# Two stacked models on one core: gates and branches of the first model computed by token, their bias rows loaded by DMA, the mix turned by feature

## The reference

```
proj = rms_norm(h) @ w_in[l]            # ..., gate_pre: 3 x 1024 columns
y_a = dsa_attention(...); y_b = short_conv_mixer(...); y_c = rwkv7_time_mix(...)
up    = einsum('bsgc,gcd->bsgd', stack([y_a, y_b, y_c]), w_branch[l])   # 512 -> 1024, three times
gates = sigmoid(gate_pre + b_gate[l])                                    # three gates of 1024
mixed = sum(gates * up, over the three branches)
h = h + mixed @ w_out[l]
h = h + conv_glu_ffn(rms_norm(h), ...)
```

## Time and profile before

| | |
|---|---|
| median of three runs | 1637.47 us |
| the profiled execution | 1637.91 us, span 1636.0 us |
| TensorE busy | 1620.9 us, 99% |
| VectorE busy | 1233.5 us, 75% |
| ScalarE busy | 966.8 us, 59% |
| POOL busy | 384.9 us, 24% |
| chain that ended last | TensorE 77%, VectorE 16%, ScalarE 4% |
| slabs | 143 of the first model, 104 of the second, median 4.9 us to landing |

### The profile page before, as it was taken

The page is one execution under the profiler, slowest core; times in us unless marked ns, Lnnn a source line. Parts: engine busy times, 40 slices in busy tenths (PEclk is TensorE's granted clock), DMA queues, the critical chain, the costliest instruction groups (busy, mean ns, idle before and its releaser), DMA issues.

```text
span 1636.0 us, 27673 instructions
## 1 busy us (share of the span) xinstructions
PE 1620.9 (99%) x11270; PEld 1409.2 (86%) x11270; DVE 1233.5 (75%) x1663; ACT 966.8 (59%) x1525; POOL 384.9 (24%) x291
## 2 busy tenths in 40 slices
PE   9999999999999999999999999999999999999998
PEld 7989999988888989999988888778788888787786
DVE  7987447699988975547799887779866668788664
ACT  7684525556567575345655574565684555656753
POOL 0663400000001945100000006508200056083000
PEclk9999999999999999999999999999999999999999
DMA  7443633455545424525465555434445555345352
GB/s 279 170 155 110 194 105 134 176 184 193 191 173 203 159 104 157 166 90 185 147 230 183 203 172 196 172 129 158 160 146 181 185 199 176 130 154 175 134 180 77
DMA packets 49182, 270.63 MB, mean 165 GB/s; under 512 B 13664, under 2 KB 14688, under 8 KB 17312
## 3 DMA queue, kind: packets, MB, share of 16 engines
q1 hardware_dynamic: 38736, 265.71, 46.5%
q10 hardware_dynamic: 9712, 2.62, 0.7%
q0 software_dynamic: 608, 0.53, 0.2%
HBM read 267.01 MB, written 1.84 MB: 164 GB/s over the span
## 4 chain that ended last, share of the span: by engine, by line
PE 77%; DVE 16%; ACT 4%; issue 2%; DMA 1%; SPq 0%; DVEq 0%; ACTq 0%
PE bank L1812 11%; PE bank L1813 11%; PE bank L1817 11%; PE bank L1704 7%; DVE w_low L1076 6%; PE bank L2866 6%; PE bank L1749 5%; PE bank L1750 5%; PE bank L1754 5%; PE bank L1709 3%; PE bank L2871 3%; PE bank L2904 2%; ACT w_high L621 1%; ACT arena L722 1%; DVE arena L1275 1%
## 5 line engine op out<-in xcount | busy, mean ns | idle before, releaser
L1076 DVE TENSOR_TENSOR w_low<-slab,w_high 128x2048 fp32r<-128x2048 f32 (+1 forms) x249 | 595.8, 2401 | 170.2 <-ACT w_high L621 163.1
L621 ACT ACTIVATE w_high<-slab 128x2048 fp32r<-128x2048 f32 (+1 forms) x249 | 470.6, 1896 | 106.5 <-PE bank L1817 88.6
L1812 PE MATMUL bank<-w_high,act 128*128 128x512 f32 x864 | 343.7, 398 | 1.4 <-DVE act L1239 0.7
L1813 PE MATMUL bank<-w_high,act 128*128 128x512 f32 x864 | 337.1, 390 | 0.0
L1749 PE MATMUL bank<-act,w_high 128*128 128x256 f32 x1024 | 258.7, 290 | 0.0
L1750 PE MATMUL bank<-act,w_high 128*128 128x256 f32 x1024 | 251.8, 283 | 0.0
L1817 PE MATMUL bank<-w_low,act 128*128 128x512 f32 x864 | 240.9, 389 | 0.0
L2416 POOL TENSOR_TENSOR arena<-arena 128x512 f32<-128x512 f32 x32 | 60.6, 1894 | 626.3 <-DVE arena L2685 626.3
L1749 PEld LDWEIGHTS bank<-act,w_high 128*128 128x128 f32 x1024 | 195.8, 191 | 8.3 <-issue 5.6
L1750 PEld LDWEIGHTS bank<-act,w_high 128*128 128x128 f32 x1024 | 196.2, 192 | 0.5 <-issue 0.5
L1812 PEld LDWEIGHTS bank<-w_high,act 128*128 128x128 f32 x864 | 162.4, 188 | 39.7 <-issue 7.4
(11 more groups left out here) (271 smaller groups left out, 2336.9 us busy)
## 6 DMA issues: line engine op xcount, KB each, us to landing
slab<-stream_a SPq DMA_DIRECT2D x143, 1024.0 KB, 4.9
slab<-stream_b SPq DMA_DIRECT2D x104, 1024.0 KB, 4.9
arena<-x_t SPq DMA_DIRECT2D x4, 256.0 KB, 6.6
slab<-stream_a ACTq DMA_DIRECT2D x2, 512.0 KB, 6.1
residual<-x_tok SPq DMA_DIRECT2D x1, 1024.0 KB, 11.5
lora_weights<-lora SPq DMA_DIRECT2D x2, 512.0 KB, 7.9
lora_weights<-final_rows SPq DMA_DIRECT2D x2, 512.0 KB, 5.9
d_inverse<-arena ACTq DMA_DIRECT2D x2, 256.0 KB, 2.2
```

The costliest lines, as they stand in the source:

```text
L621: line.did(eng.activation(core.wh[u % PARTS][:, 0:SLAB_WIDTH[u]], core.slab[u % SLABS][:, 0:SLAB_WIDTH[u]], ACT.Copy), core.sem("slab_high"))
L1076: line.did(line.eng.tensor_tensor(core.wl[u % PARTS][:, 0:SLAB_WIDTH[u]], core.slab[u % SLABS][:, 0:SLAB_WIDTH[u]], core.wh[u % PARTS][:, ...
L1812: eng.matmul(out, core.xh[:, at, columns_], wh[:, k, :], start=first and k == 0, stop=False, skip_group_check=True)
L1813: eng.matmul(out, core.xl[:, at, columns_], wh[:, k, :], start=False, stop=False, skip_group_check=True)
```

## The change

- Gate and branch slabs hold a block of 512 features by rows (`rows_by_block`) and are multiplied by token (`tokens_half`, as `out_half` does). Two gate slabs, half of the depth each, make a pair (six pairs per layer, `GATE_BLOCKS`) with two banks; a branch slab has its whole depth of 512 and two banks.
- By token the bias is a row. Six times per layer SyncE loads the pair's row, repeated over the partitions (256 KB), into the first half of `lora_weights`, behind the slab that comes five after the pair's first (`gate_rows_to`), once the last pair's banks are emptied.
- VectorE adds bank and row into the arena (`bias`), 128 x 512 twice per pair. For five of the six pairs this is the second slab's unit step, and its slab is now in `late`: the addition stands in front of the round and split two on. The first pair's is put behind mask 3.
- ScalarE's sigmoid is a step of its own (`gate`), arena to arena, 128 x 512 twice per pair.
- VectorE's products and sums of the branches keep their number and size.
- The mix is by token and is turned: TensorE turns 4 groups of 4 tiles (`mix`), two groups amid br2's second slab and two amid out's first; ScalarE and VectorE write high and low from the banks. `by_depth` is left to the FFN.

```
+BIASED = [(kind, 2 * half + 1) for kind, half in GATE_BLOCKS[1:]]
+
+
 def plan(units):
 
...
-        fills = 2 - 2 * i if kind in ("q", "w") else 2 if kind.startswith("br") else 0 if kind in ("down", "out") else 1
-        parts = 1 if kind == "up" else 1 + i if kind in ("q", "w") else 1 + i % 2 if kind == "out" else 4 if (kind, i) == ("down", FT // 2 - 1) else max(fills, 1)
-        reader = "act" if kind in ("q", "w", "rz", "ga", "gb", "gc") else "dve"
+        fills = 2 - 2 * (i % 2) if kind in ("q", "w") + GATES else 2 if kind.startswith("br") else 0 if kind in ("down", "out") else 1
+        parts = 1 if kind == "up" else 1 + i % 2 if kind in ("q", "w") + GATES else 1 + i % 2 if kind == "out" else 4 if (kind, i) == ("down", FT // 2 - 1) else max(fills, 1)
+        reader = "act" if kind in ("q", "w", "rz") else "dve"
         first = product
         banks = []
...
     put(("ga", 0), ("chunk", 0), ("mask", 0), ("chunk", 1), ("mask", 1))
-    put(("ga", 1), ("chunk", 2), ("mask", 2), ("chunk", 3), ("mask", 3), ("blocks_out", 0), ("tok", 0), ("keys", 1), ("clear", 0),
+    put(("ga", 1), ("chunk", 2), ("mask", 2), ("chunk", 3), ("mask", 3), ("bias", 0), ("blocks_out", 0), ("tok", 0), ("keys", 1), ("clear", 0),
         ("blocks_turn", 0))
-    put(("ga", 2), ("invert", 0), ("tok", 1))
+    put(("ga", 2), ("gate", 0), ("invert", 0), ("tok", 1))
     put(("ga", 3), ("tok", 2))
     amid(("gb", 0), ("flip", 0))
-    put(("gb", 0), ("off_diag", 0), ("bonus_shift", 0))
+    put(("gb", 0), ("gate", 1), ("off_diag", 0), ("bonus_shift", 0))
+    put(("gb", 2), ("gate", 2))
     amid(("gb", 2), ("blocks_in", 0))
     put(("gb", 3), ("solve", 0))
     amid(("br0", 0), ("solve", 1))
-    put(("br0", 0), ("solve", 2))
+    put(("br0", 0), ("gate", 3), ("solve", 2))
     amid(("br0", 1), ("solve", 3))
     put(("br0", 1), ("scan_rhs", 0))
     for c, unit in enumerate((("br1", 0), ("br1", 1), ("gc", 0), ("gc", 1))):
         amid(unit, ("scan_sa", c))
         put(unit, ("scan_y", c), *([("scan_rhs", c + 1)] if c < NCH - 1 else [("gn", 0), ("root_table", 0)]))
     amid(("gc", 2), ("gn", 1))
-    put(("gc", 2), ("gn", 2))
-    amid(("br2", 1), ("mix", 0))
-    put(("br2", 1), ("mix_low", 0))
+    put(("gc", 2), ("gate", 4), ("gn", 2))
+    put(("br2", 0), ("gate", 5))
+    amid(("br2", 1), ("mix", 0), ("mix", 1))
+    amid(("out", 0), ("mix", 2), ("mix", 3))
     amid(("out", 2), ("x_ffn", 0), ("x_ffn", 1))
     put(("out", 3), ("root_table", 0), ("square", 0), ("square", 1), ("norm", 1))
     amid(("up", 0), ("x_ffn", 2), ("x_ffn", 3), ("begin", UA["up", 1]), ("spread", 1))
@@ -472,7 +479,7 @@
     put(("down", FT // 2 - 2), ("root_table", 0))
     amid(("down", FT // 2 - 1), ("x_next", 0), ("x_next", 1))
     return woven(UNITS_A0 if first else UNITS_A, first, lead_steps(first), after, mid, early=[("br2", 0), ("br2", 1)],
-                 late=[("br2", 1)] + [("w", 1)] * first, behind_mid=[("q", 0), ("gc", 2)] + [("w", 0)] * (not first))
+                 late=BIASED + [("br2", 1)] + [("w", 1)] * first, behind_mid=[("q", 0), ("gc", 2)] + [("w", 0)] * (not first))
 
 
...
+def gate_rows_to(core, eng, layer, p):
+
+    stage = f"a{layer}"
+    if p == 0:
+        eng.wait_ge(core.sem("rates_made").sem, START[stage].get("rates_made", 0) + 4)
+    else:
+        kind, half = GATE_BLOCKS[p - 1]
+        for b, reader, n in PLAN_A[UA[kind, 2 * half]][4]:
+            eng.wait_ge(core.sem(f"{reader}_emptied{b}").sem, START[stage].get(f"{reader}_emptied{b}", 0) + n)
+    eng.dma_start(core.lora[:, 0:BLOCK], core.dram["gate_rows"][layer, p]).then_inc(core.sem("lora_in").sem, 16)
+
+
+def lora_loads(layer, p=-1):
+
+    return 16 * (7 * layer + p + 2)
+
+
+def gate_half(core, p, m):
+
+    kind, half = GATE_BLOCKS[p]
+    return by_token(core, GA_ if kind == "ga" else GB_, m)[:, BLOCK * half:BLOCK * half + BLOCK]
+
+
...
+        for layer in range(LAYERS):
+            for p, (kind, half) in enumerate(GATE_BLOCKS):
+                if u == FIRST_SLAB[f"a{layer}"] + UA[kind, 2 * half] + 5:
+                    gate_rows_to(core, eng, layer, p)
...
-        elif kind in ("ga", "gb", "gc"):
-            made(core, eng, rows, u)
-            g = "abc".index(kind[1])
-            if kind == "gc":
-                eng.wait_ge(*sem("summed").upto(4))
-            for k in range(2):
-                act(flat(core, (GA_ if g == 0 else GB_) + 2 * i + k), bank[banks[0][0]][:, k * T:k * T + T],
-                    ACT.Sigmoid, sem(f"act_emptied{banks[0][0]}") if k else None,
-                    bias=vec[:, VA["b_gate"] + 8 * g + 2 * i + k:][:, 0:1])
-        elif kind == "br2":
-            for k in range(i, 2):
-                mixed_high(2 * i + k)
         elif kind == "up":
             ffn(i)
 
-    def mixed_high(n):
-        eng.wait_ge(*sem("summed").upto(4 + n + 1))
-        act(core.xh[:, 8 + 2 * n:][:, 0:2, :], core.a(GA_ + 2 * n, 2), ACT.Copy, sem("mix_high"))
+    def gate(p):
+        kind, half = GATE_BLOCKS[p]
+        for m in range(2):
+            b, reader, n = rows[UA[kind, 2 * half]][4][m]
+            eng.wait_ge(*sem(f"{reader}_emptied{b}").upto(n))
+            x = gate_half(core, p, m)
+            act(x, x, ACT.Sigmoid, sem("gated") if m else None)
+
+    def mix(n):
+        eng.wait_ge(*sem("merged_turned").next(eng))
...
+        elif (kind, i) in BIASED:
+            bias(GATE_BLOCKS.index((kind, i // 2)))
         elif kind in ("br0", "br1", "br2"):
             g = int(kind[2])
-            for k in range(2):
-                at = 4 * i + 2 * k
-                src = flat(core, (GA_ if g == 0 else GB_) + at, 2)
-                if i == 0 and k == 0:
-                    emptied(core, eng, rows, UA["g" + "abc"[g], 3])
-                made(core, eng, rows, u, k)
-                did(tt(src, bank[banks[k][0]][:], src, ALU.mult), sem(f"dve_emptied{banks[k][0]}"))
+            eng.wait_ge(*sem("gated").upto(2 * g + i + 1))
+            for m in range(2):
+                part = gate_half(core, 2 * g + i, m)
+                made(core, eng, rows, u, m)
+                did(tt(part, bank[banks[m][0]][:], part, ALU.mult), sem(f"dve_emptied{banks[m][0]}"))
                 if g:
                     line.settled()
-                    did(tt(flat(core, GA_ + at, 2), flat(core, GA_ + at, 2), src, ALU.add), sem("summed"))
-                if g == 2 and i + k == 1:
-                    for at_ in ((0, 2) if i == 0 else (at,)):
-                        low(8 + at_, 2, core.a(GA_ + at_, 2), "mix_high", "mix_ready")
...
-    def mix_low(_):
-        low(14, 2, core.a(GA_ + 6, 2), "mix_high", "mix_ready")
+    def bias(p):
+        kind, half = GATE_BLOCKS[p]
+        u = UA[kind, 2 * half]
+        eng.wait_ge(sem("lora_in").sem, lora_loads(layer, p))
+        for m in range(2):
+            b = rows[u][4][m][0]
+            made(core, eng, rows, u + 1, m)
+            did(tt(gate_half(core, p, m), bank[b][:], core.lora[:, 0:BLOCK], ALU.add), sem(f"dve_emptied{b}"))
+
+    def mix(n):
+        low(8 + 2 * n, 2, heads(bank[MIX_BANK[n]], T), "mix_high", "mix_ready")
 
...
+
+MIX_BANK = (7, 6, 5, 7)
...
+    def tokens_half(u, m):
+
+        kind, i, _, _, fills = rows[u]
+        branch = kind.startswith("br")
+        if m == 0:
+            eng.wait_ge(sem("slab_high").sem, first + u + 1)
+        starts, ends = branch or i % 2 == 0, branch or i % 2 == 1
+        b, reader, _ = (fills if starts else rows[u - 1][4])[m]
+        if starts:
+            banks.fill(b, reader)
+        wh, wl = (w[(first + u) % PARTS][:].rearrange("p (k n) -> p k n", k=4) for w in (core.wh, core.wl))
+        ats = [lambda k=k: inputs[kind](i, k if branch else k + 4 * (i % 2)) for k in range(4)]
+        last = gemm_tokens(core, eng, core.bank[b][:], ats, m, wh, wl, starts, ends, None if m else first + u)
+        if ends or m:
+            last.then_inc(sem("products").sem, 1)
+
...
             return up(u)
-        if (kind, i) in (("br2", 0), ("up", 0), ("up", 1)):
+        if kind in GATES or kind.startswith("br"):
+            for m in range(u in begun, 2):
+                tokens_half(u, m)
+            return
+        if (kind, i) in (("up", 0), ("up", 1)):
...
+    def mix(n):
+        eng.wait_ge(*sem("summed").upto(4 + 2 * (n // 2) + 2))
+        banks.hold(MIX_BANK[n], "mix_ready", sem("mix_ready").upto(n + 1)[1])
+        for j in range(2):
+            for m in range(2):
+                ins = eng.transpose(bank[MIX_BANK[n]][:, j * T + m * P:][:, 0:P], by_token(core, GA_, m)[:, T * n + P * j:][:, 0:P],
+                                    core.const("ident"))
+        ins.then_inc(sem("merged_turned").sem, 1)
+
...
-            if kind in start:
+            if kind in GATES:
+                s = rows_by_block(w_in[layer], i % 2, start[kind] + BLOCK * (i // 2))
+            elif kind in start:
                 s = tiles(w_in[layer], [start[kind] + 256 * i, start[kind] + 256 * i + P])
...
```

(33 more changed lines are left out.)

30 lines of the change are left out of this document (9 added, 21 removed).

## The result

The changed kernel takes 1641.16 us (median of 16 runs, 1640.23 to 1642.49) where the kernel before takes 1637.65 (16 runs, 1637.17 to 1639.05): a ratio of 1.0021 [1.0014, 1.0028], so it is slower by 3.5 us. Forecast were 1635.9 and "no change". The profiled execution took 1642.48 us, its span is 1640.7.

What follows compares the result with a forecast made beforehand. TensorE was taken as the bound. Per layer 5.1 us saved, less 1.6 (rows, ScalarE), 1.74 (turns) and 0.95 (mix waits), left 0.8; both layers 1.6, from 1637.91 to 1636.3, less 0.4 for the median: 1635.9, range 1631.3 to 1641.5.

Steps and rivals of the forecast that it cites:

- the landing of the fourth bias rows: 256 KB load before bias 3, the addition for gb2 and gb3: lands 5.1 us from issue, bounds 4.5 to 6.2.
- the ring: VectorE and SyncE wait for each other in turn: split, slab, rows, addition, split; late loads chain.
- hidden by 0.25: Before solve 2: VectorE's additions end at 199.6, TensorE wants them at 199.85; each microsecond of later landing costs twice.
- The seam: Halves of slabs enclosed by small fp32 products: 0.18 us extra carried over unchanged, bounds 0.1 to 0.2.
- Rival S: Named with the experiments, no chance given: the wide products save less than the prediction took.
- rival C: Wide products save nothing, their pitch being twice 0.120: 5.1 us becomes 0, time 1646.1; chance 0.03.
- The stall of gb2: TensorE waits 1.5 us before gb2's second half, until the first addition of bias 2 ends at 181.8.
- Solve 0: First solve step after the gate slabs: starts at 190.05 where it was 190.35.
- The mix: By-token mix per layer: turns add two groups of eight at 0.87 (1.74 us); TensorE waits 0.6 and 0.35 for VectorE.
- ScalarE's table load: Moves from 142.24, where hidden, to gate 0 near 160.6: 1.28 us, tok 1's copies 1.6 us later.
- B: Bias rows chain: every load 1.5 us later (6.6 from issue), scan 2.7 us per layer later, 1641.3; chance 0.15.
- A: Gain stays: rows land with their slab, ScalarE absorbs the load, mix waits 0.5; 2.7 per layer, 1632.1; chance 0.27.

Runs made afterwards that it cites:

- split first: Changed kernel with the five bias additions put behind the round and split of the slab two on: 1647.07 us, 1.0055 of the kernel before.
- its repeat: The changed kernel run again unaltered, for its spread and clock: 1641.39 us, 1.0022 of the kernel before.
- early table: Changed kernel with a one-column sigmoid behind ga0, so ScalarE's table is loaded early: 1640.37 us, 1.0013 of the kernel before.
- the run without rows: Changed kernel with the twelve loads of bias rows left out, additions reading what lies in the tile: 1634.48 us, 0.9979 of the kernel before.

## Why the prediction was wrong

**The step that failed is a term of the sum: the landing of the fourth bias rows.** Its estimate put the wait of solve 2 at nothing. The mechanism was in the text (the ring of split, slab, rows, addition, split; "hidden by 0.25; each microsecond more of landing costs here twice"), and the chain of waits above runs through just those steps, at the predicted times up to the slab (bias 2 at 181.0 predicted and 180.95 measured, the slab at 186.9 and 186.99). Then the rows took 7.7 us and not 5.1. Over the 0.25 us of cover that leaves 2.3, and solve 2 came 2.1 late in layer 1; in layer 2, with 6.7 us, 0.8. Both landings lie above the bounds of 4.5 to "6.2 and a little above" that the text gave.

What differs ahead of the load is seen in SyncE's timeline of the changed kernel:

```profile
171.58 4.17 SPq L533 DMA_DIRECT2D slab<-stream_a  x2
175.85 0.38 SPq L545 DMA_DIRECT2D lora_weights<-gate_rows  x1
184.79 2.53 SPq L533 DMA_DIRECT2D slab<-stream_a  x2
187.42 0.38 SPq L545 DMA_DIRECT2D lora_weights<-gate_rows  x1
```

The x2 are two slabs each: 3.8 us from issue to issue ahead of the third rows, 2.2 us ahead of the fourth. The prediction's own list has the two splits at 184.6 and 186.8, so the two slabs could be seen; it took the landing from a row at 834 us, far from this stretch. The DMA traffic of the two stretches (first 173 to 183 us, then 185 to 197; GB/s in 40 slices, then issues with KB and us to landing):

```profile
GB/s 197 66 229 360 393 459 426 393 492 393 262 131 0 229 131 33 66 360 360 426 393 393 492 393 426 369 303 385 410 418 401 254 49 0 0 0 0 0 48 18
...
slab<-stream_a SPq DMA_DIRECT2D x1, 1024.0 KB, 4.9
lora_weights<-gate_rows SPq DMA_DIRECT2D x1, 256.0 KB, 5.1
```

```profile
GB/s 84 34 98 226 85 67 384 437 410 437 437 437 413 196 243 292 113 355 437 437 464 410 410 437 260 376 294 55 27 7 27 20 0 0 0 0 0 0 0 0
...
slab<-stream_a SPq DMA_DIRECT2D x2, 1024.0 KB, 6.4
lora_weights<-gate_rows SPq DMA_DIRECT2D x1, 256.0 KB, 7.7
...
arena<-d_inverse POOLq DMA_DIRECT2D x4, 16.0 KB, 5.1
```

In the first the traffic stops (0 GB/s) between two slabs; in the second two slabs and the rows go in one run with a dent to 113, while 16 KB pieces of the inverse blocks are fetched beside them. The landings of all runs, by what was ahead:

| ahead of the rows on SyncE's queue | inverse pieces beside them | loads | landing, us |
|---|---|---|---|
| last slab 3.6 to 4.0 us before (fourth rows two slabs early; second rows one slab early) | for the fourth, in part | 12 | 2.5 to 3.1 |
| a slab right ahead (all rows but the fourth) | no | 90 | 4.9 to 5.6 in 83, 6.1 to 6.6 in 7 |
| one slab right ahead (fourth rows one slab early) | yes | 8 | 6.2 to 7.3 |
| two slabs 3.4 us apart (split first) | yes | 2 | 6.7, 7.2 |
| two slabs 2.2 us apart, layer 1 (changed kernel, its repeat, early table) | yes | 3 | 7.7, 8.0, 7.9 |
| the same, layer 2 | yes | 3 | 6.7, 6.5, 6.8 |

All sixteen loads in this place with a slab right ahead took 6.2 us or more, and 83 of 90 elsewhere 5.6 or less, mostly 5.0 to 5.2: the place costs about 1 us and more. That the inverse pieces are the reason is not shown, since they were not varied alone and seven loads without them took over 6 us too. Nor is it shown that the second slab close ahead costs anything: in layer 2 such loads took no longer than those behind one slab. In layer 1 they took 1 us more, and why stays open. In the changed kernel the slab ahead (186.99) was itself late: it took 7.4 us, where the one ahead of the third rows took 4.9, and the rows landed 0.7 us behind it.

**The seam was mis-sized**: carried over unchanged at 0.18 per enclosed half. The enclosed half takes 2.95 and not 2.90. From its first wide product to the second are 0.43 us, 0.20 over the pitch of 0.227, and it was 0.20 over the pitch before as well (0.32), so the extra 0.05 doesn't lie there, and where it lies was not looked for. Each such half saves 0.12 and not 0.16. With 14 of them per layer this is 0.56 us a layer; the third line of the table of stages, off by 0.54, has eleven of them. Rival S is true to this extent, 1.1 us in all.

The chain of the run without rows, a half between two solve steps:

```profile
193.22 2.01 PE bank L2265 x64
195.23 0.43 PE bank L1867
...
198.18 1.83 PE bank L2265 x57
```

**The clock was not thought of.** It cost 1.55 us in the profiled execution, and nothing in that of the repeat.

**Not thought of either**: ga2 starts 0.25 us later than forecast (153.76), all of it lost before chunk 0, and 0.2 more is lost between out1 and chunk 0 of layer 2 (3.40 us behind the kernel before, then 3.60). No run looked into that; in the profiles of the experiments and the repeat chunk 0 of layer 1 starts anywhere from 136.36 to 137.15, so part of it is spread.

The difference of the spans, predicted 1634.4 and measured 1640.7, adds up to: waits of solve 2 2.9, clock 1.55, halves 1.1, late starts 0.5, turns 0.2, less 0.2 on gb2 and 0.3 on the mix's waits; together 5.8 of 6.3. The last 0.5 are not assigned.

**What held.** The pitch of 0.227 and the 24 products of a slab (rival C is out; the Trainium skill's N / 2.4 + 2.5 ns of TensorE: Matmul & The Clock Gate, Back-to-back issue gap, 216 ns for 512 columns, stays 5% under this kernel's rows). The stall of gb2: 1.5 predicted, 1.2 and 1.6 measured. Solve 0 at 190.08 for 190.05, which is in part luck: the late start and gb2's shorter wait cancel. The mix: waits of 0.7 and 0.95 in the two layers for 0.95, turns of 0.85 and 0.79, with their seam 0.94 and 0.88, for 0.87. ScalarE's table load is where it was said to be, and what it costs is in this timeline:

```profile
160.30 1.28 ACT L756 ACT_TABLE_LOAD   x1
161.60 1.16 ACT L756 ACTIVATE arena<-arena 128x512 f32<-128x512 f32 x2
```

The load starts 0.01 us behind the round before it (158.37 for 1.92), and the sigmoid 0.02 us behind the load. A drain of 1380 ns beside the load (the Trainium skill, ScalarE: Activation LUTs, What ACT_TABLE_LOAD costs) is not seen; the prediction's sum, made with the 1.28 of the row, is the right one.

**The rivals.** B is what happened: it named "bias 3 starts after 194" as its mark (195.10), and 1641.3 as its time. Its path was a little different: it had every load late by 1.5, and only the fourth was, by 2.6 and 1.6. It got 0.15, and the reason against it, "5.1 for the same size", is the mis-sized term. That its time is met within 0.2 us is luck: its waits come to 5.4 us for both layers, those beyond the forecast to 2.7 (2.9 at solve 2, less 0.2 at gb2), and clock, halves and starts, which it did not have, make up the rest. A's 1632.1 is what the same change gives with its rows in time and the mix's splits moved (1632.5 to 1632.9), by other means than A thought.

## What to carry to other kernels

The landing of a small load belongs to its place (what was issued just ahead, what runs beside it) and not to its size: 256 KB took from 2.5 to 8.0 us here, so take it from the nearest row of any size, with a margin for what the change itself issues ahead of it. Where a load that VectorE needs is issued behind a transfer that VectorE's own split releases, the two form a ring, and delays in it don't hide; issue such a load one step earlier than the last moment, at one digit of a schedule. When a term is said to be hidden by 0.25 us and its input to have bounds 1.7 us apart, the chance belongs to the side on which the cover is gone.

## What the runs showed of the hardware that was not expected

- A wait of TensorE of 2.0 us (2.4 from start to start) was followed by half the granted clock for 3.4 us in one execution and by the full clock in another of the same program. Half clock was also seen behind waits of 2.50 (split first) and 2.61 (early table) from start to start; behind those of 1.4 to 2.2 in the profiled executions it was not.
- A half of 12 products of 512 columns enclosed by small fp32 products takes 0.23 us more than one that isn't (2.95 and 2.72), a half of 24 products of 256 columns 0.18 (3.06 and 2.88).
- 256 KB landed in 2.5 to 3.1 us when nothing had been issued on its queue for 3.6 us or more, mostly in 4.9 to 5.6 right behind a slab, and in 6.2 to 8.0 right behind a slab in the stretch of the inverse pieces.
